# Square sums of five norms in column groups of 32, folded by one product with ones

## The reference, cut to what matters

```python
def rms_norm(x, g):
    xf = x.astype(jnp.float32)
    y = xf * lax.rsqrt(jnp.mean(xf * xf, axis=-1, keepdims=True) + EPS)
    return (y * g.astype(jnp.float32)).astype(x.dtype)
```

## Time and profile before

| | us |
|---|---|
| median of 3 runs | 1344.89 (1344.15 to 1345.02) |
| the profiled execution | 1340.3 |
| its span | 1338.6 |
| PE busy in it | 1312.0 (98%) |
| DVE busy | 950.7 (71%) |
| ACT busy | 652.7 (49%) |

### The profile page before, as it was taken

How to read it: one execution, slowest core, us unless ns; L and a number is a source line. 1 busy time by engine, 2 the same in 40 slices (tenths; PEclk the granted TensorE clock), 3 DMA queues, 4 the chain that set the end, 5 groups by cost and what they waited for, 6 DMA issues and landing times.

```text
span 1338.6 us, 25008 instructions
## 1 busy us (share of the span) xinstructions
PE 1312.0 (98%) x10701; PEld 1256.9 (94%) x10701; DVE 950.7 (71%) x1215; ACT 652.7 (49%) x859; POOL 78.7 (6%) x131
## 2 busy tenths in 40 slices
PE   8999999999999999999999999999999999999998
PEld 7999999998899999999988589999999878999998
DVE  5779897764776777677776878877789676754443
ACT  4644445553434433443657647444455455564442
POOL 4013000000000000020100000100000000000000
PEclk9999999999999999999999999999999999999999
DMA  9665645544387778875632046999875421455550
GB/s 283 196 201 188 189 142 192 184 128 153 103 284 269 266 277 282 275 272 176 205 125 95 2 157 214 337 314 318 314 235 166 142 84 43 163 183 182 189 187 32
DMA packets 172610, 259.24 MB, mean 194 GB/s; under 512 B 5141, under 2 KB 147778, under 8 KB 172514
## 3 DMA queue, kind: packets, MB, share of 16 engines
q1 hardware_dynamic: 160906, 203.13, 46.3%
q0 software_dynamic: 10768, 53.43, 11.2%
q10 hardware_dynamic: 840, 1.28, 0.3%
HBM read 256.77 MB, written 1.05 MB: 193 GB/s over the span
## 4 chain that ended last, share of the span: by engine, by line
PE 87%; DVE 8%; ACT 3%; issue 2%; DMA 1%; SPq 0%; ACTq 0%; DVEq 0%
PE ring L677 61%; PE acc L677 23%; ACT w_hi L1433 1%; DVE w_lo L1957 1%; DVE arena L2006 1%; PE acc L1237 1%; PE ring L1054 1%; ACT arena L1433 1%; DMA raw<-in_w_in_dram 1%; DVE h_lo L2002 0%; ACT h_hi L1433 0%; DVE stat L2560 0%; DVE stat L2561 0%; DVE h_lo L2000 0%; DVE norm L1972 0%
## 5 line engine op out<-in xcount | busy, mean ns | idle before, releaser
L677 PE MATMUL ring<-h_hi,w_hi 128*128 128x256 f32 (+1 forms) x2016 | 574.4, 285 | 4.7 <-DVE w_lo L1957 1.8
L677 PE MATMUL ring<-h_hi,w_lo 128*128 128x256 f32 (+1 forms) x2016 | 568.9, 282 | 0.0
L677 PE MATMUL ring<-h_lo,w_hi 128*128 128x256 f32 (+1 forms) x2016 | 567.2, 281 | 0.0
L1957 DVE TENSOR_TENSOR w_lo<-raw,w_hi 128x2048 fp32r<-128x2048 f32 x191 | 435.9, 2287 | 184.7 <-ACT w_hi L1433 184.1
L1433 ACT ACTIVATE w_hi<-raw 128x2048 fp32r<-128x2048 f32 x191 | 363.4, 1905 | 143.4 <-PE ring L677 74.5
L677 PEld LDWEIGHTS ring<-h_hi,w_hi 128*128 128x128 f32 x2016 | 380.6, 189 | 10.2 <-issue 5.9
L677 PEld LDWEIGHTS ring<-h_lo,w_hi 128*128 128x128 f32 x2016 | 381.4, 189 | 2.5 <-issue 2.2
L677 PEld LDWEIGHTS ring<-h_hi,w_lo 128*128 128x128 f32 x2016 | 381.7, 189 | 0.0
L677 PE MATMUL acc<-e_hi,w_hi 128*128 128x256 f32 x768 | 216.6, 282 | 0.5 <-DVE e_lo L2657 0.4
L677 PE MATMUL acc<-e_lo,w_hi 128*128 128x256 f32 x768 | 215.0, 280 | 0.0
L677 PE MATMUL acc<-e_hi,w_lo 128*128 128x256 f32 x768 | 215.0, 280 | 0.0
(11 more groups left out here) (315 smaller groups left out, 1368.0 us busy)
## 6 DMA issues: line engine op xcount, KB each, us to landing
arena<-in_w_ada_dram POOLq DMA_DIRECT2D x64, 768.0 KB, 6.1
raw<-in_w_mlp_in_dram SPq DMA_DIRECT2D x32, 1024.0 KB, 5.4
raw<-in_w_mlp_out_dram SPq DMA_DIRECT2D x32, 1024.0 KB, 4.9
raw<-in_w_in_dram SPq DMA_DIRECT2D x24, 1024.0 KB, 5.7
raw<-in_w_e_gate_dram SPq DMA_DIRECT2D x16, 1024.0 KB, 5.5
raw<-in_w_e_up_dram SPq DMA_DIRECT2D x16, 1024.0 KB, 5.4
raw<-in_w_e_down_dram SPq DMA_DIRECT2D x16, 1024.0 KB, 4.9
raw<-in_diff_w_in_dram SPq DMA_DIRECT2D x12, 1024.0 KB, 5.1
```

What stands on the lines that cost most here:

```text
L677: return nc.tensor.matmul(dst, lhs, rhs, start=start, stop=stop, **kw)
L1957: tt(w_lo[q % RAW][:, 0:n], raw[q % RAW][:, 0:n], w_hi[q % SPL][:, 0:n].bitcast(F32), ALU.subtract)\
```

## The change

The squares are summed in two steps. `group_sums` replaces `stat_pair` and `stats` for five norms: block k goes with a [128, 32] slice of ones to the 32 output rows of group k % 4, so four blocks go to four different column groups, and blocks 4 to 7 are added on top of 0 to 3. ACT copies the bank to `norm[:, 1, :]` (`fold_copy`), and one fp32 product with the full ones (`fold`) adds up the 128 rows; as each group's sum stands in 32 equal rows, the root divides by 32 * D. The places move, too: for `x`, `m0`, `m1` blocks 0 to 3 are summed after panel 2 of the projection, blocks 4 to 7 after block 3 of `raw_first`, and the fold stands after block 6; for `d` after blocks 1, 4 and 7; for `mem` all eight stand where they stood, and the fold follows the two `c_x` panels. In both perceptrons the split that stood between the take of panel 0 and `chunk_lo(0)` now stands ahead of `inverse`. Some semaphores share a number, which moves nothing.

```diff
@@ raw_first (PE) @@
-                    for j in sums.get(k, ()):
-                        stat_pair(tag, j)
+                    if k in sums:
+                        group_sums(tag, sums[k])
+                    if k == fold_at:
+                        fold(tag)
                 last.then_inc(S("panel_done"), 1)
...
+            def group_sums(tag, blocks, src=lambda k: blk(SQX, 8)[:, k]):
+
+                f = FL[tag + "_stat"]
+                if blocks[0] == 0:
+                    open_fill(f)
+                for k in blocks:
+                    if k % 2 == 0:
+                        pe.wait_ge(*sig(tag + "_squared", k // 2 + 1))
+                    g = k % 4
+                    last = mm(bank(f)[32 * g:32 * g + 32, 0:T], ones[:, 0:32], src(k), k < 4, k >= 4, skip_group_check=True)
+                if blocks[-1] == KB - 1:
+                    last.then_inc(S(tag + "_grouped"), 1)
+
+            def fold(tag):
+
+                pe.wait_ge(*sig(tag + "_folded", 1))
+                mm(bank(FL[tag + "_stat"])[:, T:2 * T], ones[:], norm[:, 1, :], True, True).then_inc(S(tag + "_summed"), 1)
...
-            stats("mem", lambda k: blk(SQ + k)[:, 0], "mem_squared")
+            group_sums("mem", range(0, 8), lambda k: blk(SQ + k)[:, 0])
             for name in ("c_x", "c_c", "c_b", "u_pool"):
                 full(name)
+                if name == "c_x":
+                    fold("mem")
...
-                stat_pair("x", i - 1)
+                if i == 2:
+                    group_sums("x", range(0, 4))
...
-                (raw_next if i else raw_first)("x", PN["x_q"] + i, half_bank(x_q_fill(i)), *(() if i else ({3: (3,)},)))
+                (raw_next if i else raw_first)("x", PN["x_q"] + i, half_bank(x_q_fill(i)), *(() if i else ({3: range(4, 8)}, 6)))
...
-                raw_first(f"m{l}", PN[name], lambda b: acc[b], {3: (3,)})
+                raw_first(f"m{l}", PN[name], lambda b: acc[b], {3: range(4, 8)}, 6)
...
-            raw_first("d", PN["d_q"], lambda b: acc[b], {1: (0, 1), 3: (2,), 4: (3,)})
+            raw_first("d", PN["d_q"], lambda b: acc[b], {1: range(0, 4), 4: range(4, 8)}, 7)
...
@@ raw_act (ACT) @@
                 func(note[:, 15:16], ones[:, 0:1], ACT.Sqrt)
+                fold_copy(tag)
                 if behind is not None:
                     ahead(behind)
-                root(tag)
+                root_folded(tag)
...
+            def fold_copy(tag):
+
+                act.wait_ge(*sig(tag + "_grouped", 1))
+                func(norm[:, 1, :], bank(FL[tag + "_stat"])[:, 0:T], ACT.Copy).then_inc(S(tag + "_folded"), 1)
+
+            def root_folded(tag):
+                f = FL[tag + "_stat"]
+                act.wait_ge(*sig(tag + "_summed", 1))
+                func(norm[:, 1, :], bank(f)[:, T:2 * T], ACT.Sqrt, scale=1.0 / (32 * D), bias=eps[:])\
+                    .then_inc(S(f"drained{f % BANKS}"), 1)
...
             ahead(PN["a_val"] + 1)
-            root("mem")
+            fold_copy("mem")
             for i in range(2):
                 take("c_x", i, blk(CX, 4)[:, 2 * i:2 * i + 2])
+            root_folded("mem")
...
@@ mlp (DVE) @@
                 name = f"mlp{l}"
+                ahead(PN[name] - 1)
                 inverse(f"m{l}")
                 chain.settle()
...
                 take(0, lambda b: acc[b])
-                ahead(PN[name] - 1)
                 chunk_lo(0)
```

More of the change, by code:

```diff
@@ L267, in program @@
         sems = {}
-        SHARED = {"squared": (4, ("x", "ffn", "f", "m0", "d", "m1")), "summed": (1, ("x", "ffn", "n", "f", "m0", "d", "m1")),
+        SHARED = {"squared": (4, ("x", "ffn", "f", "m0", "d", "m1")), "summed": (1, ("mem", "x", "ffn", "n", "f", "m0", "d", "m1")),
+                  "grouped": (1, ("mem", "x", "m0", "d", "m1")), "folded": (1, ("mem", "x", "m0", "d", "m1")),
                   "scaled": (KB, ("ffn", "n", "m0", "d", "m1")), "hi": (KB, ("ffn", "n", "m0", "d", "m1")),
@@ L273, in program @@
                   "raw_ready": (KB, ("x", "m0", "d", "m1")), "raw_taken": (2, ("m0", "d", "m1")),
+                  "exp": (1, ("group", "expert", "cmp", "lam")),
                   "input_used": (KB - 1, ("gates", "x", "m0", "d", "m1"))}
@@ L729, in linear_first, with raw_first @@
                             last.then_inc(S("panel_done"), 1)
-            def raw_first(tag, p, dst, sums):
+            def raw_first(tag, p, dst, sums, fold_at=None):
                 open_panel(p)
@@ L1292, in _ @@
                     linear_last("m0", PN["n_o"] + i, FL["n_o"] + i)
-                stat_pair("m0", i - 1)
+                if i == 2:
+                    group_sums("m0", range(0, 4))
             def mlp(l):
@@ L1413, in _ @@
                     linear_last("m1", PN["d_o"] + i, FL["d_o"] + i)
-                stat_pair("m1", i - 1)
+                if i == 2:
+                    group_sums("m1", range(0, 4))
             mlp(1)
@@ L2328, in _ @@
             tt(R(32, 4), sel, over4(m), ALU.subtract).then_inc(S("expert_logits"), 1)
-            dve.wait_ge(S("group_exp"), 1)
+            dve.wait_ge(*sig("group_exp", 1))
             step(nc.vector.tensor_reduce(R(64, 1), R(24, 4), AXX, ALU.add))
-            dve.wait_ge(S("expert_exp"), 1)
+            dve.wait_ge(*sig("expert_exp", 1))
             ex = R(36, 4)
@@ L2583, in _ @@
             n_max(0)
-            dve.wait_ge(S("cmp_exp"), 1)
+            dve.wait_ge(*sig("cmp_exp", 1))
             step(nc.vector.tensor_reduce(z, p_cmp[:, :, :, 0:NC], AXX, ALU.add))
@@ L2764, in _ @@
             d_max(1)
-            dve.wait_ge(S("lam_exp"), 1)
+            dve.wait_ge(*sig("lam_exp", 1))
             step(tt(lam[:, 2:3], lam[:, 1:2], lam[:, 0:1], ALU.subtract))
```

## The result

The changed kernel is slower: 1348.51 us median of 11 runs (1347.02 to 1351.16) against 1344.69 of the kernel before (1342.54 to 1346.81, 11 runs). The ratio is 1.0031, 95% interval 1.0021 to 1.0040, so 2.8 to 5.4 us. Forecast were 1345.9 and a range of 1340.5 to 1349.0.

A forecast was written before the change was run, and what follows sets the result against it. PE, busy 1312.0 of 1338.6 us, was taken as the bound; 7.8 us saved there against new waits, five norms summing to +1.0 us, added to the median 1344.89, gave 1345.9, range 1340.5 to 1349.

The forecast's parts named there:

- The prices of the new sums: On PE, a batch of four blocks costs 0.76 us, of eight 1.19, the fold 0.43; 7.8 saved in all.
- The rival of dearer drains: Going in and out of column groups costs more between fp32r products: total +3.6, 1348.5 us; chance 0.12.
- groups that don't overlap: With ones as weights, sums as dear as before and late roots on top: above 1350 us; chance 0.02.
- mem: Norm mem: PE waits 2.35 us for the split of panel 7, against 1.82 saved: +0.5.
- PE is full on both sides: Argument against a clock fall at the 2.35 us wait in mem: PE has full work around it.
- the clock rival: TensorE falls to its lower clock level at the new stall in mem: +2.7, 1347.6 us; chance 0.06.
- x: Norm x: PE waits for the last squares, yet raw_first ends at 270.5 instead of 270.95: -0.4 us.
- m0: First perceptron's norm: later fold and reciprocal delay the take of panel 0 and the second down: +1.7 us.
- d: Norm d: split_norm and takes 1.85 us late; rotate_d(0) waits for ACT's scaled copy: +0.3 us.
- m1: Second perceptron's norm: raw_first ends 1.5 us earlier, DVE's chain keeps its time: -1.1 us.
- The sum: Five norms, 0.5 - 0.4 + 1.7 + 0.3 - 1.1 = +1.0 us, own range -2 to +3.
- same: Whole kernel: no change beyond the 0.2% (2.7 us) a measurement can tell; chance 0.65.

The follow-up runs named there:

- e3: Changed kernel with six fp32 products of no use to the result put where PE waits ahead of the second c_c panel: 1347.11 us, 1.0016.
- e10: Changed kernel with the folds of x, m0, m1 behind block 4 and of d behind block 5, timed again: 1343.93 us, 1.0004.
- e4: Changed kernel with norm m0 put back to pairs and a plain root, the other four norms changed: 1346.86 us, 1.0013.
- e5: Kernel before with only norm mem changed, the other norms and the perceptrons' split as before: 1347.28 us, 1.0022.
- e6: Changed kernel with the folds of x, m0, m1 behind block 4 and of d behind block 5: 1348.57 us, median of 5 runs, 1.0036.
- e8: Changed kernel with the perceptrons' split back behind the take of panel 0; one run and its profile: m0 +1.80, m1 -1.12.
- e9: The changed kernel itself once more, on one chip with the repeat of the earlier folds: 1348.55 us, 1.0023.
- e2: Changed kernel with VectorE's splits of panels 7 and 8 ahead of the reciprocal of mem: 1345.06 us, 1.0004.
- e1: Changed kernel with norm mem put back to eight ones products and the root behind them, other four changed: 1345.02 us, 0.9999.

## Why the prediction was right, and where not

**The prices of the new sums: right.** The batch of eight in `mem` costs 1.19: the product ahead of it starts at 47.64, so PE is free at 47.76, and the second behind starts at 49.07, less 0.12. The first batch in `m0` costs 0.76 between fp32r products (PE is free at 809.19, the second product behind starts at 810.07). The rival of dearer drains is refuted, and so is that of groups that don't overlap. That the median, 1348.51, is the very time this rival gave (1348.5) is chance.

**mem: wait right, price short.** PE wanted the panel 1.8 earlier and stood 2.4 for the split (66.48 to 68.92; 2.35 predicted), net +0.7 where nothing else happens (e3, e10). What failed is the last step, "PE is full on both sides" as an argument against the clock rival. The clock fell behind this stall in six of seven profiles that have it (the changed kernel, e4, e5, e6, e8, e9; not e10) and in none of the six without it or with it filled. The row of the router, had shown the price of a fall; I took the cause to be small products, and idle time does it too, at 1.5 us a fall here. The Trainium skill (TensorE: Matmul & The Clock Gate, the part on HAM oscillation) tells of waits for data that bring the clock down again and make the next work start slow. The traces agree; the waits of its example are longer, about 3 to 5 us, and here 2.3 us was enough in six profiles of seven.

**x, m0, d, m1: right in place and size.** -0.41, +1.8, +0.42 and -1.06 against -0.4, +1.7, +0.3 and -1.1. (In `d` the working has the takes 1.85 late and then adds 1.75; with 1.85 it gives +0.4.) In `m0` a second cost was not counted: its wait of 1.9 had a fall behind it in two of the six profiles that have it (e2, e3), not in the four others.

**The sum.** The five terms, measured without falls, give 0.7 - 0.4 + 1.8 + 0.4 - 1.1 = +1.4, and the timed runs at full clock say +1.55 (interval of about 0.65 either way). The falls add 1.5 x 6/7 for `mem` and 1.6 x 2/6 for `m0`, 1.8 in all, an estimate from few profiles; the runs say 2.2, or 1.3 at the rate of 0.59. Together that is 3.2 of the 3.8 measured (0.8 either way). So "same" was the likeliest case by a right sum, and the measurement lies on the other side of 0.2% because of a rival that had been given too little. That the range still holds it is in part luck: its upper end was set by the drains, which cost nothing more.

**Left open.** The other falls (at 28 us in eight profiles of thirteen, behind the router, at the attention's start with 3.4 to 10.2 us or none) vary from one execution to the next, and so do the waits at 355 and 850 us. Whether the change makes any of them likelier was not tried. e1 and e5 put `mem` at 3.5 and 3.1 us in timed medians, the profiles at 2.2. The interval of e5 (1.5 to 4.4) holds that; the difference of the means for e1 (4.1, from 2.6 on) does not, so `mem` may cost more than its stall and the fall behind it.

## What to carry to other kernels

Cheaper work on the engine that bounds helps only where nothing later than it is in the way: here five norms saved 7.8 us on PE and lost it, and more, to roots that came later by the fold's place and to the falls of the clock behind the waits. Move the engines' own queues along with the dependency (splits ahead of the reciprocal that now waits, the high part ahead of the copy, and the fold itself earlier), and 7 us come back, of which about 3 are a gain on the kernel before, less than half of the 7.8. A stall of TensorE of about 2 us has a second price, half of the slow stretch behind it; count that in, with a chance.

## What the runs showed of the hardware

- Behind a wait of PE of 2.3 us in the midst of full work the granted clock was 0.5 for a stretch of 3.4 us in six of seven profiles. Behind one of 1.9 us (at `m0`) that was so in two of six, behind one of 1.8 us (at 25 to 27 us) in eight of twelve, behind one of 2.4 us (at 355 us, for `route`) in three of three, and behind one of 1.4 us (at about 165 us) in none of thirteen. Filled with six products of no use, the first had no such stretch behind it in the one profile taken.
- With ones as weights, four column groups of 32 between fp32r products of 128 columns cost 0.76 us for four sums of 256 columns and 1.19 for eight; 0.33 of each is the way in and out, as in the earlier trace rows.
- One us of (1 - c) x time goes with 0.59 us of time, not 1, among 87 runs of one kernel. Splitting a run's time by its mean clock therefore gives the clock's part as a bound, 2.2 us here, and not as a price.
